# Row sums on VectorE in place of TensorE matmuls for the conditioning of a two-block transformer

## Chip, cores and metric

One NeuronCore of a Trainium2 chip runs the whole program in one launch. The metric is the device time of one execution, in microseconds; the number shown for a kernel is the median of its runs.

## The reference, cut to what matters

A first block of two layers (feed-forward, a mixer, feed-forward) works on 256 tokens of 1024 features. A second block of two layers works on the same tokens and on 256 context tokens. Its norms and gates are modulated by a conditioning vector, one for the tokens (`c`) and one for the context (`c_ctx`):

```python
def adaln(cond, w, b, n_chunks):
    return jnp.split(jax.nn.silu(cond) @ w + b, n_chunks, axis=-1)
...
for layer in range(DEPTH):
    sh1, sc1, g1, sh2, sc2, g2 = (m[:, None, :] for m in adaln(c, w_mod[layer], b_mod[layer], 6))
    ...
    h_ctx = rmsnorm(ctx, norm1_g[layer]) * (1 + csc1) + csh1
    ...
    x = x + g1 * mix_lat
    x = x + g2 * channel_mixer(rmsnorm(x, norm2_g[layer]) * (1 + sc2) + sh2, ...)
```

`w_mod` is [2, 1024, 6144] in fp32, 50 MB in all. Both conditioning vectors and the context are inputs, so none of the modulation and nothing of the context's first norm but its shift and scale depends on the first block. The context's vectors are not needed for the second half of layer 1 (tiles 16 to 47 of that layer).

## The kernel before

Activations lie transposed in SBUF, features on partitions: `X` and `C` are eight tiles of 128x256. Every weight is streamed in units of 128x1024 fp32 (512 KB). SP's queue loads them in the order of use into 11 slots (`raw`, `load`, L526), up to 11 units ahead. ScalarE copies a unit into its high part `whi` (6 slots, `upto`, L1383), VectorE subtracts for the low part `wlo` (`upto`, L1872), and TensorE does three products of high and low parts. So a unit passes through four engines, each in its own fixed program order, tied by semaphores. ScalarE and VectorE run five or six units ahead of TensorE at most.

A feed-forward has 22 steps. In step f TensorE does the units gate f, up f and down f-2 (`FFN`, `ffn`, L756); two more down units end it. VectorE's part is `hidden` (L960): per step it sums the halves of the gate product, splits one unit, writes the low part of the previous product (`low`), then sums the halves of the up product, multiplies, and splits two units:

```python
dve.wait_ge(weight_used, p + n)
sum_halves(gs[:, f % 2, 0:T], 2 * f % 3).then_inc(halves_taken, 1)
upto(p + n + SPLIT - 1)
if f >= 1:
    low(f - 1)
...
upto(p + n + SPLIT + 1)
```

The line numbers of `hidden` in the profile are L1960 and on, those of `low` L1969, of the sums L1965, of the product L1992. The stages follow each other as ("ffn1", 0), ("in", 0), ("out", 0), ("ffn2", 0), the same with 1, then c0 and x0 (the second block's layer 0 mixers of context and tokens), ffc and ffx (its feed-forwards), c1in, x1in and the rest of x1, and last the experts (L1213), which nothing here touches. Between two stages stands a norm (`norm`, L727 on TensorE, L1402 on ScalarE, L1890 on VectorE): ScalarE squares eight tiles, TensorE sums them over partitions, ScalarE takes the root, VectorE inverts it and scales. In ("ffn2", l) the taps of a long filter are computed besides, in 17 steps that go from engine to engine (`filter_step`, L1049, L1581, L2142); GpSimd loads its tables behind the first unit (`filter_tables`, L624).

Modulation (`modulate`, L734) is a product on TensorE with the two conditioning vectors as the stationary operand `CS` and w_mod as the moving one, in 6 groups of 16 tiles of 128x1024. SP's queue loads the tiles among the weights (`mods`, L542). Group 0 and group 2 run around the norm behind ("ffn1", l), group 1 around that in front of ("ffn1", 1), group 3 at the end of the first block, group 4 inside ffc (after up 13 and up 20), group 5 inside ffx (after up 13) and behind c1in. ScalarE copies each group's rows to `MR` (`rows_out`, L1421), TensorE turns them with four transposes (`turn_rows`, L745) and VectorE adds the bias (`take_rows`, L1914).

The first block ends with its final norm of `X`. Then `scales` computes the gains, and `mix2("c0")` begins with the norm of `C`, whose output its first unit needs tile by tile. In ffc and ffx the norm of the next input is done in passing (`side_step`, L1433, L1948): ScalarE squares in steps 1 to 8, GpSimd adds the eight tiles into one (`fold`, L637), TensorE sums that over partitions after up 9 (`side_sum`, L752).

## Time and profile before

| | |
|---|---|
| runs shown | 3026.64, 3025.33, 3030.46 us; median 3026.64 |
| profiled execution | 3028.71 us, span 3026.9 us |
| granted TensorE clock, mean | 0.989 |
| busy share: TensorE, VectorE, ScalarE, GpSimd | 97%, 73%, 57%, 2% |
| read from HBM | 684.86 MB |
| w_mod loads | 96 of 512 KB, on SP's queue |

Times are microseconds from the first instruction of the profiled execution. The difference between its span and its own time lies before the first and after the last instruction. PE is TensorE, PEld its weight load, DVE VectorE, ACT ScalarE, POOL GpSimd. A busy time of PE counts pipelined matmuls, whose ends are modelled, so it tells whether the engine had work and not how fast it worked. The first 36% of the span is the first block; the experts begin at about 2255 us.

### The profile page before, as it was taken

The numbers are of one execution on the slowest core, as the hardware profiler recorded it, in microseconds if no ns is written. First come the engines' busy times: TensorE is split into PE (matmuls) and PEld (weight loads), VectorE is DVE, ScalarE is ACT, GpSimd is POOL, SyncE is SP. The second block draws the span as 40 slices with busy tenths as digits, with TensorE's granted clock in tenths as the row PEclk, the third lists the DMA queues.
The fourth block names the chain that finished last, engine by engine and source line by source line (L and its number), as shares of the span: only waits on it lengthen the run. The fifth ranks groups of instructions, "written<-read, shape, count | busy, mean of one in ns | idle before, by whom it ended". The sixth has DMA issues, their size and how long they took to land.

```text
span 3026.9 us, 50706 instructions
## 1 busy us (share of the span) xinstructions
PE 2930.8 (97%) x18747; PEld 2566.4 (85%) x18747; DVE 2213.8 (73%) x2981; ACT 1722.7 (57%) x2379; POOL 75.4 (2%) x103
## 2 busy tenths in 40 slices
PE   8999999999999999999999999999989999999998
PEld 7989788899888888789889888997978888888887
DVE  6667666666677666566676767765678999999998
ACT  4446544444555345445544444455468788878886
POOL 2000000000000000000000000000000000000000
PEclk9999999999999999999999999999999999999999
DMA  8864465886536593565386776745559999999999
GB/s 248 276 184 140 116 194 175 260 276 184 163 117 182 159 288 92 147 178 153 93 250 183 225 237 184 224 110 149 169 196 363 366 355 363 366 362 358 364 364 336
DMA packets 664466, 692.13 MB, mean 229 GB/s; under 512 B 22830, under 2 KB 518146, under 8 KB 663009
## 3 DMA queue, kind: packets, MB, share of 16 engines
q1 hardware_dynamic: 658432, 665.06, 68.7%
q0 software_dynamic: 5712, 24.54, 2.2%
q8 instruction: 124, 2.03, 0.3%
q14 instruction: 54, 0.43, 0.1%
q10 hardware_dynamic: 144, 0.07, 0.0%
HBM read 684.86 MB, written 4.72 MB: 228 GB/s over the span
## 4 chain that ended last, share of the span: by engine, by line
PE 88%; DVE 6%; ACT 3%; issue 2%; DMA 1%; DVEq 0%; SPq 0%; ACTq 0%
PE W L693 35%; PE ACC L693 20%; PE W L786 16%; PE W L787 8%; PE W L686 4%; PE ACC L686 3%; DVE wlo L1877 2%; ACT whi L1390 1%; PE ACC L1000 1%; PE W L1210 1%; DMA scratch<-in_w_mod 1%; PE ACC L1201 0%; DVE R L1896 0%; DVE M L2030 0%; DVE gs L1965 0%
## 5 line engine op out<-in xcount | busy, mean ns | idle before, releaser
L1877 DVE TENSOR_TENSOR wlo<-raw,whi 128x1024 fp32r<-128x1024 f32 (+3 forms) x681 | 765.5, 1144 | 360.1 <-ACT whi L1390 358.1
L1390 ACT ACTIVATE whi<-raw 128x1024 fp32r<-128x1024 f32 (+3 forms) x681 | 655.5, 985 | 52.0 <-PE W L693 33.2
L2386 DVE TENSOR_TENSOR wlo<-raw,whi 128x1024 fp32r<-128x1024 f32 x528 | 617.5, 1219 | 43.5 <-ACT whi L1746 34.6
L786 PE MATMUL W<-HB,whi 128*128 128x512 f32 x1760 | 635.6, 403 | 14.0 <-DVE HB L1899 14.0
L1746 ACT ACTIVATE whi<-raw 128x1024 fp32r<-128x1024 f32 x528 | 547.4, 1060 | 94.6 <-PE W L693 52.4
L787 PE MATMUL W<-HB,wlo 128*128 128x256 f32 x1760 | 497.1, 282 | 0.0
L693 PE MATMUL W<-HB,whi 128*128 128x256 f32 x2592 | 479.4, 287 | 13.8 <-DVE HB L1899 8.0
L693 PE MATMUL W<-whi,HB 128*128 128x512 f32 (+1 forms) x1664 | 478.7, 373 | 4.9 <-issue 3.5
L693 PEld LDWEIGHTS W<-HB,whi 128*128 128x128 f32 x2592 | 407.1, 193 | 22.1 <-issue 12.7
L786 PEld LDWEIGHTS W<-HB,whi 128*128 128x128 f32 x1760 | 333.4, 189 | 103.1 <-issue 19.7
L1460 ACT ACTIVATE sg<-gs 128x256 f32<-128x256 f32 x132 | 55.1, 418 | 591.4 <-DVE gs L1965 591.4
L693 PE MATMUL W<-HB,wlo 128*128 128x256 f32 x1296 | 368.2, 284 | 0.0
L693 PEld LDWEIGHTS W<-whi,HB 128*128 128x128 f32 x1664 | 300.1, 189 | 60.3 <-DVE wlo L2386 4.4
L787 PEld LDWEIGHTS W<-HB,wlo 128*128 128x128 f32 x1760 | 336.1, 191 | 0.0
L693 PE MATMUL W<-wlo,HB 128*128 128x512 f32 (+1 forms) x832 | 307.7, 370 | 0.0
L693 PE MATMUL ACC<-hhi,whi 128*128 128x256 f32 x1056 | 303.9, 288 | 0.0
L693 PE MATMUL ACC<-hlo,whi 128*128 128x256 f32 x1056 | 298.9, 283 | 0.0
L693 PE MATMUL ACC<-hhi,wlo 128*128 128x256 f32 x1056 | 298.8, 283 | 0.0
L693 PEld LDWEIGHTS W<-HB,wlo 128*128 128x128 f32 x1296 | 250.3, 193 | 0.0
L1965 DVE TENSOR_REDUCE gs<-W 128x256 f32<-128x512 f32 x132 | 91.0, 689 | 162.2 <-PE W L787 162.1
L693 PEld LDWEIGHTS ACC<-hhi,whi 128*128 128x128 f32 x1056 | 200.6, 190 | 10.3 <-issue 4.8
L693 PEld LDWEIGHTS ACC<-hlo,whi 128*128 128x128 f32 x1056 | 200.8, 190 | 2.4 <-issue 2.4
(459 smaller groups left out, 4042.8 us busy)
## 6 DMA issues: line engine op xcount, KB each, us to landing
raw<-in_moe_w_gate SPq DMA_DIRECT2D x183, 512.0 KB, 5.3
raw<-in_moe_w_up SPq DMA_DIRECT2D x180, 512.0 KB, 5.4
raw<-in_ffn_w_in SPq DMA_DIRECT2D x176, 512.0 KB, 3.9
raw<-in_moe_w_down SPq DMA_DIRECT2D x176, 512.0 KB, 5.5
raw<-in_w_in SPq DMA_DIRECT2D x105, 512.0 KB, 4.8
raw<-in_ffn_w_out SPq DMA_DIRECT2D x88, 512.0 KB, 3.6
scratch<-in_w_mod SPq DMA_DIRECT2D x60, 512.0 KB, 7.4
raw<-in_mix_w_in SPq DMA_DIRECT2D x48, 512.0 KB, 3.7
```

The source lines that it names most:

```text
L686: return mm(o, a, b, start=start, stop=stop, skip_group_check=True)
L693: last = mm(o, a, b, start=start and i == 0, stop=stop and i == 2, skip_group_check=True)
L786: mm(o, wh[:, w], both(k), start=k == 0, stop=False, skip_group_check=True)
L787: last = mm(o[:, 0:T], wl[:, w], high[:, k, :], start=False, stop=k == KT - 1, skip_group_check=True)
L1000: last = nc.tensor.transpose(bank(4 + b % 2)[:, w], P2[:, (4 * i + b) % 3, w], ident[:, :])
L1210: last = nc.tensor.transpose(W[:, 2 * (g % 2), at], hdt[:, g % 2, at], ident[:, :])
L1390: A_(whi[:, g % SPLIT, 0:LONG[g]], raw[:, g % RAW, 0:LONG[g]], ACT.Copy).then_inc(weight_high, 1)
L1460: A_(sg[:, f % 2, 0:T], gs[:, f % 2, 0:T], ACT.Silu).then_inc(gated, 1)
L1746: A_(whi[:, g % SPLIT, :], raw[:, g % RAW, :], ACT.Copy).then_inc(weight_high, 1)
L1877: V.tensor_tensor(wlo[:, g % RAW, 0:LONG[g]], raw[:, g % RAW, 0:LONG[g]], whi[:, g % SPLIT, 0:LONG[g]].bitcast(F32), ALU.subtract).then_in ...
L1965: return V.tensor_reduce(o, W[:, b, :].rearrange("p (i t) -> p t i", i=2), AX.X, ALU.add)
L2386: V.tensor_tensor(wlo[:, g % RAW, :], raw[:, g % RAW, :], whi[:, g % SPLIT, :].bitcast(F32), ALU.subtract).then_inc(weight_split, 1)
```

## The change

w_mod comes transposed, so that a tile has 128 outputs on partitions and the 1024 inputs in the row. VectorE multiplies a tile with the conditioning vector, which stands on every partition, and sums along the row: one instruction per tile and vector. There are 96 tiles; the first 64 need both vectors, the other 32 only the tokens'. `MOD_STEPS` gives each tile a step of a feed-forward; the first half of a tile's work comes at the end of step f, the second after the gate sum of step f+1. GpSimd's queue loads the tiles into three slots, or one in ("ffn2", l), and loads the two conditioning vectors four times, since their place is used otherwise in between. ScalarE applies the Silu to them. All modulation matmuls, their row copies and transposes go.

The context's first norm moves into ("ffn2", 1): squares in steps 13 and 14, the fold on GpSimd behind the eighth tile's load, the sum after up 18, the root in step 19, the scaling in steps 20 and 21, high and low parts behind the last up unit. TensorE goes from the last down unit into c0in. The final norm of `X` moves into c0in: the squares in front, the fold on GpSimd, the sum ahead of the third unit, the scaling in units 3 to 6. The bias of layer 0 is added in step 1 of ("ffn2", 1), that of layer 1 in front of ffx and in x1in. The copy of the filter to HBM moves behind the tile loads of its stage.

```diff
+        COND = M[:, 2048:4096].rearrange("p (i k) -> p i k", i=2)
+        def mod_slot(name, i):
+            s = 0 if name in FILTERS else i % 3
+            if s == 0:
+                return s, M[:, 4096:5120]
+            return s, (G if name[0] == "ffn1" else S)[:, s * 1024:(s + 1) * 1024]
...
+        MOD_STEPS = {("ffn1", 0): range(5, 22), ("ffn2", 0): range(2, 19, 2), ("ffn1", 1): range(0, 22),
+                     ("ffn2", 1): range(2, 19, 2), "ffc": range(2, 22), "ffx": range(2, 21)}
+        COND_AT = {("ffn1", 0): 3, ("ffn2", 0): 2, ("ffn2", 1): 2, "ffc": 1}
...
@@ sync: every stream() loses its mods
-                       {RAW - 1: [(1, MODS, 16)], 24: [(2, 0, MODS)]} if l else {30: [(0, 0, MODS)]})
+                stream(("ffn1", l), ffn_units(w1, w1, FF, w2))
...
@@ gpsimd
+            def condition():
+                for i, v in enumerate((A["c_2"][0], A["c_ctx_2"])):
+                    pool.dma_start(COND[:, i, :], v.partition_broadcast(128)).then_inc(cond_in, 16)
+            def mod_tiles(name, first, last):
+                for i in range(first, last):
+                    s, dst = mod_slot(name, i)
+                    u = MOD_FIRST[name] + i
+                    if i >= (1 if name in FILTERS else 3):
+                        pool.wait_ge(mod_used, u if name in FILTERS else u - 2)
+                    elif i == 0 and u:
+                        pool.wait_ge(mod_used, u)
+                    if name == ("ffn1", 1) and i == 1:
+                        pool.wait_ge(weight_used, start[name] + 1)
+                    pool.dma_start(dst, A["w_mod_laid"][u // 48, u % 48 * 128:u % 48 * 128 + 128, :]).then_inc(mod_landed[s], 16)
...
             for l in range(2):
+                if l == 0:
+                    condition()
+                mod_tiles(("ffn1", l), 0, len(MOD_STEPS["ffn1", l]))
                 filter_tables(("ffn2", l), l)
+                condition()
+                mod_tiles(("ffn2", l), 0, 8)
+                if l == 1:
+                    fold(flat, side_squares, KT, side_folded)
+                mod_tiles(("ffn2", l), 8, 9)
+                keep_filter(l)
+            fold(flat, last_squared, KT, last_folded)
             for inst, l, full in MIXES:
                 if inst == "c1":
-                    for e in (1, 2):
-                        fold(e, TT[:, :, :].rearrange("p k t -> p (k t)"))
+                    pool.wait_ge(weight_used, start["ffc"] + 1)
+                    condition()
+                    for name in SIDE_INPUT:
+                        mod_tiles(name, 0, 10)
+                        fold(flat, side_squares, KT * SIDE[name] + KT, side_folded)
+                        mod_tiles(name, 10, len(MOD_STEPS[name]))
...
@@ tensor: ffn, mix2 and the order of the stages
                         if f == 13:
                             pe.wait_ge(side_root, e + 1)
-                            modulate(e + 3, 0, 4, W[:, 3, :])
-                        if f == 20 and name == "ffc":
-                            modulate(4, 4, KT, W[:, 3, :])
+                    if name == ("ffn2", 1) and kind == "up" and f == 18:
+                        pe.wait_ge(freq_taken, 10)
+                        side_sum(SIDE[name], W[:, 3, 0:T])
...
+                    if inst == "c0" and n == 2:
+                        pe.wait_ge(last_folded, 1)
+                        f32(ACC[:, 6, :], ones[:, :], TT[:, 0, :]).then_inc(pe_to_act, 1)
...
-                modulate(2 * l, 0, 2, W[:, 3, :])
                 norm()
-                modulate(2 * l, 2, KT, W[:, 3, :])
                 mix1(l)
                 norm(o=ACC[:, 0, :])
                 ffn(("ffn2", l))
-            modulate(3, 0, 2, W[:, 3, :])
-            norm()
-            modulate(3, 2, KT, W[:, 3, :])
+            pe.wait_ge(side_root, 1)
             mix2("c0")
...
@@ scalar: ffn and mix2
+                    if COND_AT.get(name) == f:
+                        act.wait_ge(cond_in, 32 * list(COND_AT).index(name) + 32)
+                        A_(COND[:, :, :], COND[:, :, :], ACT.Silu).then_inc(cond_ready, 1)
...
                 high(NF - 1)
+                if name == ("ffn2", 1):
+                    act.wait_ge(weight_used, p + at[("up", NF - 1)] + 1)
+                    for k in range(KT):
+                        side_high_part(SIDE[name], k)
...
                 if inst == "c0":
-                    rows_out(3, W[:, 3, :])
+                    for k in range(KT):
+                        act.wait_ge(dve_to_act, heard.next("dve_to_act"))
+                        A_(TT[:, k, :], X[:, k, :], ACT.Square).then_inc(last_squared, 1)
...
@@ vector
+            def mod_part(name, f, i):
+                if f not in MOD_STEPS[name]:
+                    return
+                j = MOD_STEPS[name].index(f)
+                u = MOD_FIRST[name] + j
+                both = u < 64
+                if i == 1 and not both:
+                    return
+                s, w = mod_slot(name, j)
+                if i == 0:
+                    dve.wait_ge(mod_landed[s], 16 * mod_load(name, j))
+                    if u:
+                        dve.wait_ge(mod_used, u)
+                    if j == 0 and name in COND_AT:
+                        dve.wait_ge(cond_ready, list(COND_AT).index(name) + 1)
+                ins = V.scalar_tensor_tensor(w if i or not both else JUNK, w, 1.0, COND[:, i, :], ALU.mult, ALU.mult,
+                                             accum_out=MOD[:, u // 48, u % 48, i:i + 1])
+                if i == 1 or not both:
+                    ins.then_inc(mod_used, 1)
...
+            def early_step(f):
+                if f == 1:
+                    add_bias(0, 0, 48, True)
+                    for w in range(2):
+                        scales(0, w)
+                if f == 20:
+                    dve.wait_ge(side_root, 1)
+                    link(V.reciprocal(R[:, :], R[:, :]))
+                if f in (20, 21):
+                    for k in range(4 * (f - 20), 4 * (f - 19)):
+                        side_scale(0, k)
...
                     sum_halves(gs[:, f % 2, 0:T], 2 * f % 3).then_inc(halves_taken, 1)
+                    mod_part(name, f - 1, 1)
                     upto(p + n + SPLIT - 1)
...
                     upto(p + n + SPLIT + 1)
+                    mod_part(name, f, 0)
                 low(NF - 1)
+                mod_part(name, NF - 1, 1)
+                if name == ("ffn2", 1):
+                    for k in range(KT):
+                        side_low(SIDE[name], k)
                 upto(p + N + AHEAD - 1)
...
+                    if n == 3 and inst == "c0":
+                        dve.wait_ge(act_to_dve, heard.next("act_to_dve"))
+                        link(V.reciprocal(R[:, :], R[:, :]))
+                    if 3 <= n < 7 and inst == "c0":
+                        for k in (2 * n - 6, 2 * n - 5):
+                            done_x = V.scalar_tensor_tensor(X[:, k, :], X[:, k, :], PV[:, 3, 74 + k:75 + k], R[:, :],
+                                                            ALU.mult, ALU.mult)
```

## Rows read from the trace of the kernel before

**Rows 1.** The page's busy line: busy us (share of the span) xinstructions.
```profile
PE 2930.8 (97%) x18747; PEld 2566.4 (85%) x18747; DVE 2213.8 (73%) x2981; ACT 1722.7 (57%) x2379; POOL 75.4 (2%) x103
```

**Rows 2.** Busy time by stretch, most of ("ffn1", 1); columns as in the first line.
```profile
core 0: us, PE busy (x) PEld busy (x) DVE busy (x) ACT busy (x) POOL busy (x), PEclk, DMA share, GB/s
586.00:772.00 186.00, 186.00 (x1227) 169.85 (x1225) 122.96 (x160) 79.98 (x113) 0.00 (x0) 1.00 0.72 220
```

**Rows 3.** Chain of waits in order of time: start, us, what.
```profile
205.65 8.63 PE ACC L693 x72
...
561.97 8.64 PE ACC L693 x72
...
763.64 8.64 PE ACC L693 x72
...
1126.37 5.52 PE W L686 x32
...
1146.69 8.81 PE W L693 x48
1155.50 0.44 PE ACC L749 x4
...
1691.88 3.57 PE W L686 x32
```

**Rows 4.** Timeline of VectorE, one step of ("ffn1", 1): start, us, what [idle before <-releaser].
```profile
675.59 0.69 DVE L1965 TENSOR_REDUCE gs<-W 128x256 f32<-128x512 f32 x1 [1.52 <-PE W L787]
677.72 1.23 DVE L1877 TENSOR_TENSOR wlo<-raw,whi 128x1024 fp32r<-128x1024 f32 x1 [1.44 <-ACT whi L1390]
...
680.26 2.35 DVE L1877 TENSOR_TENSOR wlo<-raw,whi 128x1024 fp32r<-128x1024 f32 x2
684.11 0.69 DVE L1965 TENSOR_REDUCE gs<-W 128x256 f32<-128x512 f32 x1 [1.50 <-PE W L787]
```

**Rows 5.** Timeline of TensorE, the norm in front of ("ffn2", 0), without modulation.
```profile
353.59 3.62 PE L686 MATMUL ACC<-TT,ones 128*128 128x256 f32 x16
361.17 0.77 PE L786 MATMUL W<-HB,whi 128*128 128x512 f32 x1 [3.97 <-DVE HB L1899]
...
366.79 0.40 PE L786 MATMUL W<-HB,whi 128*128 128x512 f32 x1
```

**Rows 6.** Busy time behind that norm, columns as in rows 2.
```profile
361.00:370.00 9.00, 8.83 (x35) 6.95 (x36) 6.89 (x17) 6.82 (x11) 2.75 (x6) 0.69 0.20 58
```

**Rows 7.** Timeline of TensorE behind the three norms with modulation.
```profile
226.99 0.38 PE L693 MATMUL W<-HB,whi 128*128 128x256 f32 x1
...
586.90 0.40 PE L786 MATMUL W<-HB,whi 128*128 128x512 f32 x1
...
783.74 0.39 PE L693 MATMUL W<-HB,whi 128*128 128x256 f32 x1
```

**Rows 8.** Groups by line: count, busy us, mean ns, idle before.
```profile
L1896 DVE RECIPROCAL R<-R 128x256 f32<-128x256 f32 x9 | 15.8, 1752 | 21.2 <-ACT R L1414 21.2
L2367 DVE SCALAR_TENSOR_TENSOR TT<-ACC,now,scratch 128x1024 f32<-128x1024 f32 x8 | 10.3, 1284 | 10.6 <-PE ACC L693 10.6
L1571 ACT ACTIVATION_READ_ACCUMULATOR M<-W,small 128x1 f32 x48 | 9.7, 202 | 0.0
```

**Rows 9.** Timeline of VectorE, the scaling by the final norm.
```profile
1134.21 3.25 DVE L1903 SCALAR_TENSOR_TENSOR X<-X,PV,R 128x256 f32<-128x256 f32 x8
```

**Rows 10.** Timeline: the sum after up 9 of ffc, and the fold in ffx.
```profile
1657.19 0.59 PE L686 MATMUL W<-TT,ones 128*128 128x256 f32 x2
...
1844.82 5.15 POOL L641 TENSOR_TENSOR TT<-TT 128x1024 f32<-128x1024 f32 x3 [190.76 <-ACT TT L1438]
```

**Rows 11.** Timeline of ("ffn2", 0): the table's load, the sine, a 1024-column pass.
```profile
371.99 0.59 POOL L633 DMA_DIRECT2D scratch<-in_k_dft  x1
...
383.17 0.42 ACT L1585 ACTIVATE scratch<-gscratch 64x256 f32<-64x256 f32 x1 [2.80 <-DVE gscratch L2140]
...
389.74 1.04 ACT L1588 ACTIVATE gscratch<-gscratch 128x1024 f32<-128x1024 f32 x1
```

**Rows 12.** DMA issues from 365 to 390: count, KB each, us to landing.
```profile
scratch<-in_k_dft POOLq DMA_DIRECT2D x1, 1408.0 KB, 10.6
```

More of the change, by code:

```diff
@@ L694, in mm3, with linear @@
                 return last
-            def linear(p, units, x, to, by_tile=None, group=None, off=0, free=None, ahead=None, drain=True):
+            def linear(p, units, x, to, by_tile=None, off=0, free=None, ahead=None, drain=True):
                 N = len(units)
                 for n, (kt, nn) in enumerate(units):
-                    if group is not None and n == 2:
-                        turn_rows(group, ACC4[:, 0, :])
                     if ahead is not None:
@@ L1299, in _ @@
             ffn("ffc")
-            ffn("ffx", 4)
+            ffn("ffx")
             ctx_keys_values()
@@ L1793, in _ @@
                 ffn(("ffn2", l))
-            norm(X, after="tiles", ahead=start["c0in"] + AHEAD)
             mix2("c0", 0)
@@ L2002, in summed, with ffn @@
                     dve.wait_ge(weight_used, start[name] + sizes[name])
-            def ffn(name, gate, res, group=None, tiles=True):
-                hidden(name, group)
+            def ffn(name, gate, res, tiles=True):
+                hidden(name)
                 for n in range(KT):
@@ L2328, in mix2 @@
                 if inst == "x0":
[L2329 removed]
+                    side_low(SIDE["x0"], KT - 1)
             def ctx_keys_values():
```

243 lines of the change are left out of this document (103 added, 140 removed).

## The prediction, made before the changed kernel ran

> **What bounds the kernel now.** I read the page's busy line first: TensorE is busy for 97% of the span [rows 1]. The split by stage says the same of the feed-forwards of the first block and leaves VectorE at two thirds there [rows 2]. So a microsecond taken out of TensorE's order counts where its neighbours run back to back, and VectorE has room for work, but not much more than a third of a step. Next, the chain of waits in order of time shows where modulation stands on the path: 5.52 us right at the end of the first block, and 3.57 us three times inside the second block's feed-forwards, between matmuls that wait for nothing [rows 3]. Last, the timeline of one steady step of a feed-forward gives VectorE's own schedule [rows 4]: a step is 8.52 us (675.59 to 684.11), of which VectorE waits 1.44 us for ScalarE's high part and 1.50 us for the next gate unit. That leaves 5.58 us of work. A down unit is 8.64/3 = 2.88 us [rows 3], so gate and up take 2.82 us each.
>
> **Removed: modulation between the stages.** A norm without it has a row: from 353.59 (end of the unit before) to 366.79 (end of the first unit behind it) is 13.20 us; TensorE idles 3.97 us, and the first unit behind the wait lasts 5.62 us (361.17 to 366.79), 2.8 more than the 2.82 of a steady one [rows 5]. The granted clock is 0.69 on average from 361 to 370 [rows 6]: for that unit it is at the lower of its two levels, 1.2 in place of 2.4 GHz. With modulation the same stretch runs from 214.28 to 226.99 + 2.88 = 229.87 (15.6 us), from 570.61 to 586.90 (16.3 us) and from 772.28 to 783.74 + 2.88 = 786.62 (14.3 us) [rows 3, 7]. So 2.4, 3.1 and 1.1 us come off, not the 5.5 us that TensorE spends, because most of it filled a wait of the norm, and the low clock after an idle wait is already in the 13.20. Two of the three follow a stage whose last tile has two VectorE instructions behind the last up unit; they make the residual later by about a microsecond, of which I let 0.5 us through in each. Gain 5.6 us.
>
> **Removed: modulation inside ffc and ffx.** Three pieces of 3.57 us [rows 3] with nothing idle beside them: 10.7 us. The fourth, ahead of x1in, fills a wait for the norm: nothing. The six sets of four transposes take 0.44 us on the chain [rows 3], in ffn nearer 0.36: 2.3 us. A sum added to ("ffn2", 1) costs an eighth of the norm's 3.62 us [rows 5]: -0.5 us.
>
> **The boundary to c0.** Now 1126.37 to 1155.50 holds two units (5.76 us) and 23.4 us of two norms, modulation and low clock [rows 3]. After the change the context's tiles are scaled in steps 20 and 21 of ("ffn2", 1), so c0in can follow the last down unit. Three things remain. (a) Steps 20 and 21 load VectorE with a reciprocal (1.75 us [rows 8]) and twice four scalings of 3.25/8 = 0.41 us [rows 9], ahead of the last product: step 20 has 5.58 + 1.44 + 3.4 = 10.4 us against 8.52, step 21 starts 1.9 us late and adds 1.6 us. The low part for the last down unit is ready 7.9 us behind the last up unit, and TensorE wants it at 2 x 2.88 = 5.76: 2.1 us idle. (b) The residual update of X stands on VectorE behind eight low parts, so it ends about 4.5 us after the last down unit; ScalarE squares, GpSimd folds in 5.15 us [rows 10], and TensorE waits for the fold ahead of the third unit, 5.76 us in: 10.1 - 5.8 = 4.3 us idle. (c) An idle stretch of that length cost 2.8 us of low clock behind it [rows 5], and the sum itself is 0.5. Together 9.7 us; gain 23.4 - 9.7 = 13.7 us. Scaling X afterwards lies in VectorE's gaps of c0in.
>
> **Added: 160 multiply-and-sum instructions on VectorE**, 128x1024, two per tile for 64 tiles and one for 32. No row shows one with a sum output. The nearest without is 1.28 us on 128x1024, and ScalarE's read of an accumulator is 0.20 us [rows 8], so 1.28 to 1.48 us; I take 1.3, as two subtractions of the size follow each other at 2.35/2 [rows 4]. In ("ffn1", l) the second one of a tile lands in the 1.44 us gap and the first in the 1.50 us gap [rows 4]: free up to 1.44 us, and 5.58 + 2 x 1.3 = 8.2 us of 8.52 are then filled. In ffn2 a tile comes every second step. What hides them is thus VectorE's gap alone; each 0.1 us beyond 1.5 costs 0.2 us per step in 39 steps. By the Trainium skill (Vector Engine (DVE) Microarchitecture Reference, "Points that are easy to get wrong") a scalar_tensor_tensor with two SBUF sources that aren't bf16 runs at half throughput. By that the sum would end slower; it is the last rival.
>
> **Moved: the loads, from SP's queue to GpSimd's.** 96 transfers of 512 KB as before, at about 0.6 us of issue each [rows 11]. SP's queue loses its waits, which held up no weights. On GpSimd they stand ahead of the folds, and a load waits for VectorE to free its slot. That matters once in ffc: its tenth load waits for tile 7 (step 8), whose second instruction runs in step 9, 0.7 + 1.3 us behind the end of gate 9. With the issue the fold starts 2.7 us behind that point and ends 5.15 us later, at 7.9; TensorE wants the sum right behind up 9, at 2.8. Before, the sum ran at 1657.19 without a wait [rows 10]. So 5.1 us idle and 2.8 us of low clock: -7.9 us. In ffx tiles have one instruction and the slot comes free 2.8 us earlier: -2.1 us, and no low clock. In ("ffn2", 1) the sum is asked for three steps later: 0.
>
> **Added: two broadcast loads of the conditioning vectors and a Silu of them**, four times. In ffn2 they stand behind the filter's tables on GpSimd's queue. The table issued at 371.99 takes 10.6 us to land [rows 11, 12], to 382.6, so 1 MB behind it lands near 390 at the same rate (1408 KB in 10.6 us) and near 387 if half of that time was not its own, and ScalarE, which asks for it in step 2, just behind the sine at 383.17 [rows 11], stands 4 to 6 us and then computes 2 us on 2048 columns (twice the 1.04 us for 1024 at 389.74 [rows 11]). Weight high parts queue behind it. They are five units ahead, which covers most; I take 2.5 us of TensorE idle in each of the two, from bounds of 0 (the depth covers all) and 8 (nothing). -5 us. In ("ffn1", 0) and ffc the loads have time or the delay is under the depth: 0, at most 2.
>
> **Sum.** 5.6 + 10.7 + 2.3 - 0.5 + 13.7 - 7.9 - 2.1 - 5.0 = 16.8 us. The profiled execution took 3028.71 us, span 3026.9; it would take 3011.9. The median of the runs shown is 2.07 us lower: **3010 us**.
>
> **Rivals.**
> *The waits aren't paid.* The vectors land in time, and the depth of weights takes the folds' delay at c0. Back come 5 us and some 3 of c0: 3002 us. For it: a step is 8.5 us and five units are 14. Against: GpSimd works in order.
> *VectorE a little over its step.* At 1.6 us per instruction both gaps overflow, 0.27 us per step; over 22 and 17 steps, less 0.8 us of margin at each end (the last low part is ready at 5.0 us of 5.76), 9 us: 3019 us.
> *VectorE is the bound, slower than before.* The place is ("ffn1", l) from step 5 and step 0 on. Between 256 and 1024 columns the rows give (1.28 - 0.41)/768 = 1.13 ns per column; at twice that an instruction takes 2.45 us, a step 5.58 + 4.9 = 10.5 us, 2.0 us over, 39 times 77 us, and 7 steps of ffc some 9 more: about 3096 us. It decides from 39 x (5.58 + 2c - 8.52) = 18.3 (the gain and the two margins), c = 1.70 us. Against: the scalings have two fp32 SBUF sources and take 0.41 us on 256 columns, where half rate would need 0.67.
> *It doesn't take the work away.* Nothing in the diff leaves a modulation matmul on TensorE; no chance given.
>
> **Numbers.** My forecast 0.55, waits not paid 0.17, a little over 0.17, VectorE the bound 0.08; the rest is a stall that I don't see, on either side of no change (0.03). Range 2999 to 3026: down to the unpaid waits with step 20 of ("ffn2", 1) unpaid besides, up to 1.6 us per instruction with 5 us more in ffn2 and 2 in the other stages. A measurement here can tell 0.2%, 6 us, from no change. Below 3020.6: 0.82; within: 0.08; above: 0.10.
>
> **What the profile would show.** No matmul with the conditioning operand; TensorE busy about 40 us less. The new instruction at 1.2 to 1.44 us, and gate sums of ("ffn1", 1) every 8.5 us; if they come every 9 us or more, the third rival. From the last down unit of ("ffn2", 1) to the third unit of c0in about 15 us with one idle stretch ended by ScalarE or GpSimd. An idle stretch of about 5 us ended by the fold behind up 9 of ffc, 2 us in ffx. ScalarE idle in step 2 of ffn2 until the vectors land. Wrong would be: the same distances between boundaries, or idle TensorE in steady steps.

## The result, and the profile after

The kernel after the change takes 3038.78 us (median of seven runs, 3034.53 to 3045.65), the kernel before 3026.95 us on the same chip: measured ratio 1.0043, 95% interval 1.0033 to 1.0053 (the two medians alone give 1.0039). It is 0.4% slower where I forecast 0.55% faster, and outside my range. The profiled execution is the slowest of the seven, 3045.65 us with a span of 3043.8; its span is 16.9 us longer than before's, the median 11.8, so some 5 us of what the comparison of traces shows are this execution's own.

The page's busy line after, which answers to [rows 1], and the row of its queues that grew (packets, MB, share of the DMA engines' time; 5712 packets and 24.54 MB before):

```profile
PE 2908.9 (96%) x18311; PEld 2574.4 (85%) x18311; DVE 2399.6 (79%) x3294; ACT 1727.4 (57%) x2377; POOL 143.8 (5%) x213
q0 software_dynamic: 20688, 79.07, 7.4%
```

TensorE has 436 instructions less, yet its busy time fell by 21.9 us only, where I had expected about 40, and the mean granted clock of the core went from 0.989 to 0.977. To see what that means I added up half-microsecond windows from the first weight matmul (20.5 us) to the start of the second block's expert part (2226.98 us before, 2241.24 after). Idle is the window less the busy time; "lost to the clock" is busy time times one minus the granted clock; the remainder is TensorE's work at full clock. A matmul that waits a little for its operand inside a unit counts as busy, so the lost time is an upper bound of what the clock cost; e4_clock_fill below shows a place where it cost nothing.

| us of TensorE | before | after | difference |
|---|---|---|---|
| work at full clock | 2116.4 | 2062.4 | -54.0 |
| idle | 67.9 | 106.8 | +38.9 |
| lost to the low clock | 22.2 | 51.5 | +29.3 |
| length | 2206.5 | 2220.7 | +14.3 |

So the change does what it says: 54.0 us of work are gone. 38.9 come back as waits and up to 29.3 as low clock behind them. By stretch, against my terms (plus is a gain; the lengths run from first matmul to last):

| stretch | before | after | gain | forecast |
|---|---|---|---|---|
| ("ffn1", 0) | 193.8 | 197.4 | -3.6 | 0 |
| three boundaries, last down unit to end of the next unit | 47.3 | 40.8 | +6.5 | +5.6 |
| mixing of the first block, both | 260.4 | 258.8 | +1.6 | +0.8 |
| ("ffn2", 0) | 209.4 | 215.5 | -6.1 | -2.5 |
| ("ffn1", 1) | 185.2 | 184.8 | +0.4 | +0.4 |
| ("ffn2", 1) | 209.8 | 220.8 | -11.1 | -5.1 |
| last down unit to the norm of x0 | 223.8 | 208.3 | +15.5 | +16.2 |
| x0, to ffc | 226.7 | 226.8 | 0 | 0 |
| ffc and ffx | 391.6 | 407.2 | -15.6 | +1.1 |
| the rest | | | -4.5 | +0.4 |

The waits that are new, from TensorE's timeline after: start, us, what [idle before <- releaser].

```profile
51.60 0.63 PE L826 MATMUL W<-ident,scratch 128*128 128x128 f32 x4 [2.08 <-ACT C L1490]
...
423.92 1.29 PE L711 MATMUL W<-gscratch,scratch 64*128 64x512 f32 x2 [2.98 <-DVE gscratch L2205]
...
1135.75 0.36 PE L718 MATMUL ACC<-hhi,whi 128*128 128x256 f32 x1 [2.15 <-DVE hlo L2017]
1149.45 1.22 PE L711 MATMUL ACC<-TT,ones 128*128 128x256 f32 x2 [4.84 <-POOL TT L651]
...
1661.04 0.80 PE L711 MATMUL W<-TT,ones 128*128 128x256 f32 x1 [6.96 <-POOL TT L651]
...
1771.81 0.36 PE L718 MATMUL ACC<-hhi,whi 128*128 128x256 f32 x1 [2.26 <-DVE hlo L2017]
...
1862.95 0.80 PE L711 MATMUL W<-TT,ones 128*128 128x256 f32 x1 [6.58 <-POOL TT L651]
```

There are two more like them, 4.24 us at 981.50 (the filter in the second ffn2) and 2.26 us at 1973.49 (the last down units of ffx). And the low clock behind the fold of ffc, in the busy time by stretch (us, PE, PEld, DVE, ACT, POOL, PEclk, DMA share, GB/s):

```profile
1661.00:1667.00 6.00, 5.96 (x26) 5.78 (x27) 2.21 (x3) 0.00 (x0) 0.56 (x1) 0.50 0.27 87
```

TensorE is busy for 5.96 of 6 us at the lower of its two levels, so this one wait cost 6.96 us and then about 3 more.

The new instruction in its place in ("ffn1", 1), VectorE's timeline, against [rows 4]:

```profile
686.14 0.69 DVE L2013 TENSOR_REDUCE gs<-W 128x256 f32<-128x512 f32 x1 [0.35 <-PE W L790]
686.75 1.21 DVE L1939 SCALAR_TENSOR_TENSOR gscratch<-gscratch,M 128x1024 f32<-128x1024 f32 x1
687.89 0.08 DVE L1939 DVE_READ_ACCUMULATOR gscratch<-gscratch,M 128x1 f32 x1
688.27 1.22 DVE L1886 TENSOR_TENSOR wlo<-raw,whi 128x1024 fp32r<-128x1024 f32 x1 [0.30 <-ACT whi L1389]
689.41 0.42 DVE L2017 TENSOR_TENSOR hlo<-hd,hhi 128x256 fp32r<-128x256 f32 x1
689.74 0.68 DVE L2013 TENSOR_REDUCE us<-W 128x256 f32<-128x512 f32 x1
690.46 0.43 DVE L2041 TENSOR_TENSOR hd<-sg,us 128x256 f32<-128x256 f32 x1
690.80 2.35 DVE L1886 TENSOR_TENSOR wlo<-raw,whi 128x1024 fp32r<-128x1024 f32 x2
693.08 1.22 DVE L1939 SCALAR_TENSOR_TENSOR M<-M 128x1024 f32<-128x1024 f32 x1
694.22 0.08 DVE L1939 DVE_READ_ACCUMULATOR M<-M 128x1 f32 x1
694.68 0.69 DVE L2013 TENSOR_REDUCE gs<-W 128x256 f32<-128x512 f32 x1 [0.38 <-PE W L790]
```

It takes 1.22 us and 0.08 for the read of its sum: the 1.3 us of my sum. Gate sums come every 8.54 us (686.14 to 694.68), and VectorE still waits 0.38 us for TensorE: free in a steady step of ffn1, as forecast.

### The profile page after: what moved, and what is told of

Its sections match the earlier page's. It is cut to its first block, busy times and chain, and to the rows that moved or that the text cites. A ratio compares the mean times of both kernels' runs of the same rounds, so it can differ in the third digit from the quotient of the medians.

```text
span 3043.8 us, 50209 instructions
## 1 busy us (share of the span) xinstructions
PE 2908.9 (96%) x18311; PEld 2574.4 (85%) x18311; DVE 2399.6 (79%) x3294; ACT 1727.4 (57%) x2377; POOL 143.8 (5%) x213
## 4 chain that ended last, share of the span: by engine, by line
PE 77%; DVE 12%; ACT 5%; issue 3%; DMA 1%; POOL 1%; POOLq 0%; DVEq 0%; ACTq 0%; SPq 0%
PE W L718 35%; PE ACC L718 16%; PE W L789 11%; PE W L790 6%; DVE wlo L1886 5%; PE ACC L711 3%; PE W L711 3%; ACT whi L1389 2%; DVE gs L2013 1%; DMA M<-in_c_ctx 1%; PE ACC L1001 1%; DVE M L1939 1%; PE W L1214 1%; DVE us L2013 1%; DVE hlo L2017 0%
## 5 line engine op out<-in xcount | busy, mean ns | idle before, releaser
L789 PE MATMUL W<-HB,whi 128*128 128x512 f32 x1760 | 642.7, 407 | 18.1 <-DVE HB L1908 18.0
L718 PE MATMUL W<-HB,whi 128*128 128x256 f32 x2592 | 486.3, 290 | 21.6 <-DVE HB L1908 13.4
L718 PEld LDWEIGHTS W<-HB,whi 128*128 128x128 f32 x2592 | 413.2, 196 | 28.4 <-issue 19.1
L789 PEld LDWEIGHTS W<-HB,whi 128*128 128x128 f32 x1760 | 337.1, 192 | 109.8 <-issue 24.2
L790 PEld LDWEIGHTS W<-HB,wlo 128*128 128x128 f32 x1760 | 340.5, 193 | 0.0
L718 PEld LDWEIGHTS W<-HB,wlo 128*128 128x128 f32 x1296 | 254.1, 196 | 0.0
L718 PEld LDWEIGHTS ACC<-hhi,wlo 128*128 128x128 f32 x1056 | 205.6, 195 | 0.0
```

What stands on the lines that cost most here:

```text
L718: last = mm(o, a, b, start=start and i == 0, stop=stop and i == 2, skip_group_check=True)
L789: mm(o, wh[:, w], both(k), start=k == 0, stop=False, skip_group_check=True)
L790: last = mm(o[:, 0:T], wl[:, w], high[:, k, :], start=False, stop=k == KT - 1, skip_group_check=True)
```

## The experiments

Lengths and stalls are from each kernel's trace, times are medians; 3038.78 is what they are held against, with the kernel before beside each. The single kernels scatter by about 5 us to either side from run to run, so a gain of 4 us is told from nothing only just.

**The fold in ffc and ffx.**

```diff
-                        mod_tiles(name, 0, 10)
+                        mod_tiles(name, 0, 9)
                         fold(flat, side_squares, KT * SIDE[name] + KT, side_folded)
-                        mod_tiles(name, 10, len(MOD_STEPS[name]))
+                        mod_tiles(name, 9, len(MOD_STEPS[name]))
```

> One number changes: in ffc and ffx GpSimd issues nine tile loads ahead of its fold, not ten, so the fold no longer waits for VectorE to free the slot in step 9. My theory: the two stalls ended by the fold (6.96 us at 1661.04 and 6.57 us at 1862.95) and the low clock behind them (about 3 us of TensorE's time each) are the price of that wait, so both vanish and the time falls from 3038.8 to about 3019 us (3015 to 3023). The fold starts right behind ScalarE's last square, near 1645.5, and is over before up 9 ends. Rival: the sum of VectorE's work in ffc and ffx, stretched by the folds, is what the two stages pay for; then TensorE's idle time moves to the last down units (2.26 us each now, 5 or more then) and the gain is under 8 us, 3031 us or more.

Measured: 3025.48 us, ratio 0.9999 [0.9989, 1.0009], so 13.3 us better than after: outside the theory's range, between it and the rival. Both waits for the fold are gone; GpSimd starts it at 1642.49 and ends at 1649.48. But TensorE's timeline at the end of ffc has

```profile
1760.96 0.55 PE L718 MATMUL ACC<-hhi,whi 128*128 128x256 f32 x1 [4.05 <-DVE hlo L2017]
```

where it was 2.26 us, and again in ffx. VectorE's own timeline in that kernel says why:

```profile
1659.69 0.69 DVE L2013 TENSOR_REDUCE gs<-W 128x256 f32<-128x512 f32 x1
1661.82 1.23 DVE L1886 TENSOR_TENSOR wlo<-raw,whi 128x1024 fp32r<-128x1024 f32 x1 [1.44 <-ACT whi L1389]
1662.96 0.42 DVE L2017 TENSOR_TENSOR hlo<-hd,hhi 128x256 fp32r<-128x256 f32 x1
1663.30 0.68 DVE L2013 TENSOR_REDUCE us<-W 128x256 f32<-128x512 f32 x1
1664.01 0.42 DVE L2041 TENSOR_TENSOR hd<-sg,us 128x256 f32<-128x256 f32 x1
1664.36 2.35 DVE L1886 TENSOR_TENSOR wlo<-raw,whi 128x1024 fp32r<-128x1024 f32 x2
1666.63 1.22 DVE L1939 SCALAR_TENSOR_TENSOR scratch<-scratch,M 128x1024 f32<-128x1024 f32 x1
...
1667.77 0.69 DVE L2013 TENSOR_REDUCE gs<-W 128x256 f32<-128x512 f32 x1
```

No wait for TensorE is left in this step: only the one of 1.44 us for ScalarE, which itself waits for the gate sum. The cycle is 8.08 us and doesn't get shorter, TensorE's is 8.52. What VectorE has lost it makes up at 0.44 us a step.

**The conditioning vectors.**

```diff
-("ffn2", 0): range(2, 19, 2), ... ("ffn2", 1): range(2, 19, 2)
+("ffn2", 0): range(4, 21, 2), ... ("ffn2", 1): (5, 7, 9, 11, 13, 15, 17, 18, 19)
-COND_AT = {("ffn1", 0): 3, ("ffn2", 0): 2, ("ffn2", 1): 2, "ffc": 1}
+COND_AT = {("ffn1", 0): 5, ("ffn2", 0): 4, ("ffn2", 1): 5, "ffc": 1}
```

(and GpSimd issues six tiles ahead of the fold of the second ffn2, not eight)

> The Silu of the conditioning vectors stands in step 5 of ffn1 (was 3), step 4 of the first ffn2 (was 2) and step 5 of the second (was 2); the tiles of ffn2 begin in those steps, two apart as before and one apart at the end of the second. The number of instructions is the same. My theory: ScalarE's wait for the vectors and the 1.9 us Silu in the filter's steps make VectorE late for the filter's first taps, and cost TensorE 2.07, 2.98 and 4.24 us idle (51.60, 423.92, 981.50) and some 1.7 us of low clock behind each: all three vanish, the time falls by 14 us to about 3024 us (3020 to 3028). Rival: it is VectorE's multiply-and-sum instructions in the filter's steps that make it late; they are still there, so the stalls of the two ffn2 move but stay, only the 3.8 us of ffn1 go, and the time is about 3035 us.

Measured: 3030.99 us, ratio 1.0011 [1.0001, 1.0020]; 7.8 us better, where I expected 14 and a time of 3028 at most. The filter's wait falls to 0.87 us and, in the second ffn2, from 4.24 to nothing (another, for the tap sums, grows from 0.88 to 2.04). The theory holds for both ffn2, as far as this run can tell: the edit moves the first tiles together with the Silu, so it doesn't separate the two. It was wrong for ("ffn1", 0), where 2.32 us stay at 50.68 with the Silu two steps later. In the kernel after the change ScalarE's timeline shows both causes:

```profile
38.80 1.06 ACT L1389 ACTIVATE whi<-raw 128x1024 fp32r<-128x1024 f32 x1 [2.46 <-DMA raw<-in_ffn_w_in]
...
385.30 1.91 ACT L1473 ACTIVATE M<-M 128x2048 f32<-128x2048 f32 x1 [1.48 <-DMA M<-in_c_ctx]
```

At 385.30 it stands 1.48 us for the vectors and computes 1.91: VectorE, which waits for ScalarE's next high part, is 3.4 us late and reaches the filter's taps late. The two traces separate what the run doesn't: the gate sum of the next step comes 30.3 us behind the stage's first matmul (391.62) where it came at 26.3 before (387.44), and of these 4.1 us 3.4 are ScalarE's; of the multiply-and-sum instructions only one had run by then. At 38.80 ScalarE stands for a weight.

**The start.**

```diff
                 if l == 0:
+                    pool.wait_ge(weight_used, 9)
                     condition()
```

> One wait is added to the kernel after the change: GpSimd issues the first load of the conditioning vectors and the first tiles only when TensorE has used nine weights (about 46 us in). My theory: in the first 40 us these 2.5 MB share the DMA engines with the first weights of the feed-forward, one of which ScalarE waits for (2.46 us at 38.80), and that is the stall of 2.07 us at 51.60 with 1.7 us of low clock behind it. Both go: 3038.8 less 4 us, 3035 us (3032 to 3037). The vectors land near 52 us; ScalarE asks for them in step 3, at 51.4, so up to 2 us of its time may come back. Rival: the stall is ScalarE's table or VectorE's copy and not the loads: no change, or ScalarE now waits for the vectors and the stall stays: 3037 to 3042 us.

Measured: 3044.63 us, ratio 1.0055 [1.0038, 1.0072]: 6 us worse, a miss. The first half was right: with the loads held back no weight is late, and the wait at 51.60 is gone. But now the vectors are late, issued at 48.94, and TensorE stands 7.23 us at 65.28. ScalarE's timeline:

```profile
57.10 1.91 ACT L1474 ACTIVATE M<-M 128x2048 f32<-128x2048 f32 x1 [8.35 <-DMA M<-in_c_ctx]
```

It is 8.2 us from the first issue to the last landing for 1 MB among 1.5 MB of tiles and the weights. Of ScalarE's wait of 8.35 us I had allowed 2. The start needs both, later loads and a later Silu (it has them in e8_all below). In kernels that leave the start as it is, TensorE's wait there (2.08 us at 51.60 above) is 1.1 to 3.6 us long from one execution to the next: part of the scatter of this change's times.

**Order inside VectorE's step.** In every feed-forward, on both engines:

```diff
-                    upto(p + n + SPLIT - 1)
                     if f >= 1:
                         high(f - 1)
+                    upto(p + n + SPLIT - 1)
```

(on VectorE `low(f - 1)`; its second multiply-and-sum also behind `low`, and `low(f)` of the last step ahead of its last `upto`)

> In each step of every feed-forward the split of the previous hidden tile (high part on ScalarE, low part on VectorE) comes ahead of the next weights' split, and in the last step ahead of the next stage's weights. The instructions are the same. My theory: VectorE runs one wait late at the end of ffc and ffx and of the second ffn2, which costs 2.26, 2.26 and 2.15 us of idle TensorE (1771.81, 1973.49, 1135.75) and about 2 us of low clock behind each of the first two. With the low part earlier by about 1.5 us (in the wait for ScalarE) in steps and by 2.4 us at the end these go: 3028 us (3024 to 3032). The low part fills part of the 1.43 us gap, so a step of VectorE doesn't grow. Rival: the weights' low parts, now 0.4 us later, are what TensorE waits for next, idle of 0.3 us or more appears in steady steps, and the time stays or rises (3038 to 3050 us).

Measured: 3049.5 us, ratio 1.0078 [1.0061, 1.0095]: 10.7 us worse. The aimed-at waits shrank (2.26 to 0.62, 2.15 to 0.55 us), and yet. VectorE's timeline at the end of ("ffn1", 1):

```profile
769.41 0.68 DVE L2013 TENSOR_REDUCE gs<-W 128x256 f32<-128x512 f32 x1
770.88 0.42 DVE L2017 TENSOR_TENSOR hlo<-hd,hhi 128x256 fp32r<-128x256 f32 x1 [0.79 <-ACT hhi L1457]
771.23 1.22 DVE L1939 SCALAR_TENSOR_TENSOR gscratch<-gscratch,M 128x1024 f32<-128x1024 f32 x1
```

and TensorE's behind it:

```profile
782.09 0.70 PE L711 MATMUL W<-TT,ones 128*128 128x256 f32 x2 [3.28 <-ACT TT L1409]
```

The low part now stands first in the wait for ScalarE, of which 0.79 us is idle again, and the modulation instruction that had filled it comes after: gate sums now come every 8.57 us, 760.84 to 769.41, without a wait for TensorE, where they came every 8.53 with a wait of 0.37. VectorE has become the bound, arrives late at the residual, and the next norm's squares with it. Two waits for GpSimd's fold grew as well, at c0 from 4.84 to 7.09 us and in ffc from 6.96 to 9.30; how much of the 10.7 us each accounts for isn't separated. Not the weights, as my rival had it, but VectorE's cycle: in ffn1 it has 0.37 us a step to spare and no more.

**The slot of the single instruction.** On top of e1_fold_first:

```diff
-                if i == 1 and not both:
+                if i == 0 and not both:
                     return
...
-                if i == 0:
+                if i == 0 or not both:
```

> On top of e1_fold_first: where a tile has one multiply-and-sum instruction (the later tiles of ffc, all of ffx) it stands in VectorE's wait for ScalarE's high part (1.43 us, empty there) at the start of the next step, not in the slot behind the step's last low part. My theory: with the instruction in the other slot VectorE's own cycle is 8.07 us (gate sum to gate sum back to back, 1659.69 to 1667.77 in e1_fold_first) against TensorE's 8.52, so it makes up only 0.45 us per step of what the fold and the side norm cost it, and is still 4 us late at the last down units. In the wait its cycle is 6.8 us and the two stalls of 4.05 us and the low clock behind them (2 us each) go: 3025.5 less 12 us, 3013.5 us (3010 to 3018). Rival: what makes VectorE late at the end is work near the end, not the slack of a step, or the tile isn't there in time in the earlier slot: gain under 4 us, 3021 us or more.

Measured: 3016.4 us, ratio 0.9956 [0.9939, 0.9974]: 9.1 us better than e1_fold_first, as the theory had it. VectorE's step in ffc, with side work in it:

```profile
1711.85 0.68 DVE L2014 TENSOR_REDUCE gs<-W 128x256 f32<-128x512 f32 x1
1712.45 1.22 DVE L1940 SCALAR_TENSOR_TENSOR scratch<-scratch,M 128x1024 f32<-128x1024 f32 x1
...
1713.97 1.23 DVE L1886 TENSOR_TENSOR wlo<-raw,whi 128x1024 fp32r<-128x1024 f32 x1 [0.29 <-ACT whi L1389]
...
1720.21 0.69 DVE L2014 TENSOR_REDUCE gs<-W 128x256 f32<-128x512 f32 x1 [0.55 <-PE W L790]
```

The instruction costs nothing there, and soon behind the side norm VectorE waits for TensorE again. From the second unit of ffc to x1in it is 419.8 us after the change (21.1 idle, 11.5 lost to the clock), 406.2 in e1_fold_first (10.8 and 7.6) and 392.8 here (2.7 and 3.0). With these two edits the kernel beats the one before.

**The last sum at c0.**

```diff
-                        pe.wait_ge(last_folded, 1)
-                        f32(ACC[:, 6, :], ones[:, :], TT[:, 0, :]).then_inc(pe_to_act, 1)
+                        pe.wait_ge(kept_out, 32)
+                        pe.wait_ge(last_squared, KT)
+                        for k in range(KT):
+                            last = f32(ACC[:, 6, :], ones[:, :], TT[:, k, :], k == 0, k == KT - 1)
+                        last.then_inc(pe_to_act, 1)
```

(and GpSimd's fold for it goes)

> The last sum of X's squares at the boundary to c0in is made by TensorE itself from ScalarE's eight squares (eight matmuls, 3.6 us), not from GpSimd's fold (one matmul). My theory: at 1149.45 TensorE stands 4.83 us for the fold and loses 2.8 us to the low clock; the squares are there at 1142.9, before it reaches the sum, so nothing is waited for and it pays 3.1 us more of work: 3038.8 less 4.5 us, 3034 us (3031 to 3037), and the granted clock from 1149 to 1155 is 1.0. Rival: c0in waits next for the weights' low parts, which VectorE could not split while GpSimd folded (6.50 us for three at 1143.99), or for X's scaling: no gain.

Measured: 3034.75 us, ratio 1.0025 [1.0016, 1.0035]: 4.0 us better, as expected. The eight matmuls wait for nothing, and the clock behind them stays up:

```profile
1140.00:1146.00 6.00, 6.00 (x48) 5.87 (x47) 0.34 (x1) 1.89 (x3) 0.00 (x0) 1.00 0.28 68
```

**Half of VectorE's new work in ffn1.** `mod_part` returns for the second instruction in ("ffn1", l); the context's sums aren't computed there.

> The kernel after the change with the second multiply-and-sum instruction of each tile left out in the two ffn1 (39 of 160 instructions, 1.22 us each with 0.08 us for reading the sum): the context's part of the first block's modulation and a part of the second's aren't computed. Theory (that of the prediction): in ffn1 the instruction stands in VectorE's wait for ScalarE's high part and costs TensorE nothing; only the one ahead of the residual at the end of each ffn1 is felt, by under 1 us. 3037 us (3034 to 3040), and the stage from 584 to 783 keeps its 198.7 us to within 1.5 us. Rival: VectorE is the bound in ffn1 too; the 39 instructions are 48 us of its work, and at least 10 us come off: 3029 us or less.

Measured: 3034.68 us, ratio 1.0028 [1.0018, 1.0039]: 4.1 us for 48 us of VectorE's work, and ("ffn1", 1) to the next first matmul is 197.9 us against 198.7. What is gained stands behind the last step, where the norm's wait is 3.97 us (776.75) in place of 4.73. The rival, VectorE as the bound in ffn1, falls.

**The clock.** Behind the eight matmuls of `norm`:

```diff
+                for i in range(14):
+                    f32(W[:, 3, 0:128], ones[:, :], ones[:, :])
```

> Behind the eight matmuls of each norm on the main path TensorE issues 14 matmuls 128x128 of ones on ones, into a bank that nobody reads, about 3 us of work in the 4 to 4.7 us in which it waits for the normalized tiles. Nothing of the computation changes. My theory: what modulation between the stages gave, beside its result, was a TensorE that stayed at 2.4 GHz; with the filler the low clock behind the norms of the first block and of x0 goes (1.6 us of TensorE's time near 226, 1 to 2.5 us at each of the seven places): 3038.8 less about 12 us, 3027 us (3022 to 3032), and the mean granted clock rises from 0.977 to about 0.984. Rival: the clock falls for another reason than the idle wait (the stalls inside the stages), or the filler delays the first matmul behind the norm: no gain, 3036 to 3042 us.

Measured: 3036.5 us, ratio 1.0036 [1.0021, 1.0050]: 2.3 us, less than its scatter; a miss. The clock did rise, to 0.983, and 11.0 us less count as lost to it; each of the six waits filled is 3.1 us shorter. But nothing behind them comes earlier. The first unit behind the norm ahead of ("ffn1", 1), in the kernel after the change and in this one (columns as above):

```profile
584.22:589.80 5.58, 5.48 (x17) 3.44 (x18) 4.82 (x14) 4.17 (x8) 0.00 (x0) 0.69 0.00 0
```

```profile
589.25:594.82 5.57, 4.90 (x17) 2.62 (x18) 4.81 (x14) 4.16 (x8) 0.00 (x0) 1.00 0.01 3
```

The unit takes 5.58 us at a mean granted clock of 0.69 and 5.57 at 1.00 (at all six places 5.6 to 6.0 in both kernels; ahead of the second ffn2 5.66 at 0.54 and 5.57 at 1.00). VectorE hands it its eight tiles one by one, each 0.73 us behind the last (`HB<-TT,HB` starts at 589.41, 590.14, 590.87 and so on in this kernel), and TensorE follows at that pace. So neither the wait ahead of this unit nor the low clock in it had anything to give back, and the filter's wait at 427 us grew to 4.35. Filling a wait raises the clock; that pays only where the work behind it is ready and no other engine sets its pace.

**All of it.** e1, e2, e5, e6, e7 and, in the last step of the second ffn2 alone, `low(f)` ahead of `upto`:

> All of it together: e1_fold_first, e2_cond_later, e5_gap_slot, e6_start_later, e7_c0_sum, and in the last step of the second ffn2 the low part of the hidden tile ahead of the next stage's weights (2.14 us of idle TensorE at 1133.76). Theory: the stalls are separate, so the gains add up: 13.3 + 7.8 (measured) + 12 + 4 + 4.5 + 2 = 43.6 us, 2995 us (2989 to 3003), 1.0% below the kernel before. Rival: they hide one another, VectorE being near its bound in the first block too; then under two thirds of the sum arrives, 3010 us or more.

Measured: 2997.93 us, ratio 0.9896 [0.9879, 0.9912]: 40.9 us below the kernel after the change, of 43.6 summed. The 43.6 were in part expectations: what e1, e2, e5 and e7 measured adds up to 34.2, and the rest is the start, which needed both edits, and `low(f)`, which no run tried alone. No sign that the stalls hide one another. The same accounting gives 2066.0 us of work, 76.1 idle and 35.9 at most lost to the clock.

Two additions to it: twelve fillers behind each norm, and the last tile's second instruction of each ffn1 behind the residual.

> e8_all with twelve filler matmuls (ones on ones, 128x128, into a bank that nobody reads) behind each norm on the main path. Theory: in e4_clock_fill the filler brought back 13 us of low clock, but half of it ran into the stalls behind (the filter's taps, 4.35 us there in place of 2.98), and two of the fourteen came too late. In e8_all those stalls are gone and twelve fit: 2997.9 less 7 us, 2991 us (2987 to 2995). Rival: the filler costs at its end what it gives back by the clock: 2996 to 3002 us.

> e8_all with the second instruction of the last tile of each ffn1 behind the residual's update of X, not ahead of it. Theory: it stands 1.22 us ahead of the residual (771.31, residual at 773.59) and the last down unit ends at 774.5, so X could be done about 1 us earlier at each of the two boundaries, and with it ScalarE's squares and TensorE's norm: 2997.9 less 2 us, 2996 us (2993 to 2999). Rival: the instruction is waited for by the next stage's weights instead: no change or 1 us more.

> e8_all, e10_all_fill and e11_all_residual in one kernel. Theory: the filler (3.9 us against e8_all) and the later instruction (2.7 us) act at the same boundaries but on different waits, the one on the clock and the other on the residual, so most of both stays: 2992 us (2989 to 2994). Rival: with X ready earlier the twelve fillers no longer fit into the wait behind the norm, and TensorE's first unit is late by what the residual won: 2994 to 2996 us, no better than either alone.

Measured: 2993.98 us (0.9888 [0.9873, 0.9903]) with the fillers, 2995.28 us (0.9892 [0.9877, 0.9907]) with the later instruction, and 2993.98 us (0.9888 [0.9872, 0.9905]) with both, as e12_best's rival had it: together they are no better than the fillers alone. All three are within 2 us of each other and 2.7 to 4.0 below e8_all, and the intervals of all four overlap, so none of these additions is told from nothing. The clock of the last is 0.991, above the 0.989 of the kernel before.

## Why the prediction was wrong

*Removed work, boundaries.* Right. The three norms cost 13.90, 13.01 and 13.89 us where I had 13.20 with half a microsecond on two; gain 6.5 for 5.6. The difference lies in my reading of before: I added a steady 2.88 us for the unit behind the norm, or took the start of the next unit for its end, and got 46.2 us, where the ends of the units give 47.3. The reason that I gave for the 13.20 was wrong, though: I put the 5.62 us of its first unit down to the low clock, and it is VectorE's pace, as e4_clock_fill shows.

*VectorE's instruction.* Its length (1.30 us) and its being free in ffn1's steady steps were right; e9_half confirms it. The half rate that the Trainium skill states for two SBUF sources that aren't bf16 (Vector Engine (DVE) Microarchitecture Reference, "Points that are easy to get wrong") isn't seen here: 1024 columns in 1.22 us, against the 2.45 that my third rival built on it. That rival failed for the reason that I gave, with a slip in it: at half rate the scaling would need 0.70 us by my own slope, not 0.67.

*The boundary to c0.* Right: 15.5 us less 2.15 idle ahead of the last down unit are 13.4, forecast 13.7. Of its terms (a) was 2.1 and is 2.15; (b) was 4.3 and is 4.84 here, 3.4 in five of the other kernels that leave this place alone. (c) was 2.8 and 2.8 are lost there, but by luck: the row that I took it from shows VectorE's pace. e7_c0_sum took (b) and (c) away for 4.0 us.

*The fold in ffc and ffx: the step that failed first.* "In ffx tiles have one instruction and the slot comes free 2.8 us earlier: -2.1 us, and no low clock." In ffc the start was right to 0.2 us, and in ffx the slot does come free 2.2 us earlier (2.84 us ahead of TensorE's stop at 1856.37, 0.66 in ffc). What I had wrong is the length: the fold takes 7.0 us in ffc and 8.8 in ffx, not the 5.15 of [rows 10], which I had taken as fixed. GpSimd's and VectorE's timelines in ffc after the change:

```profile
1653.42 0.53 POOL L645 DMA_DIRECT2D M<-in_w_mod_laid  x1 [7.99 <-DVE M L1939]
1653.96 2.89 POOL L651 TENSOR_TENSOR TT<-TT 128x1024 f32<-128x1024 f32 x1
1658.07 2.92 POOL L651 TENSOR_TENSOR TT<-TT 128x512 f32<-128x512 f32 x2 [1.22 <-issue]
```

```profile
1654.56 2.57 DVE L2017 TENSOR_TENSOR hlo<-hd,hhi 128x256 fp32r<-128x256 f32 x1
1657.05 0.68 DVE L2013 TENSOR_REDUCE us<-W 128x256 f32<-128x512 f32 x1
1657.76 0.42 DVE L2041 TENSOR_TENSOR hd<-sg,us 128x256 f32<-128x256 f32 x1
1658.10 3.96 DVE L1886 TENSOR_TENSOR wlo<-raw,whi 128x1024 fp32r<-128x1024 f32 x2
```

and GpSimd's in ffx:

```profile
1854.08 2.42 POOL L651 TENSOR_TENSOR TT<-TT 128x1024 f32<-128x1024 f32 x1
1859.44 3.46 POOL L651 TENSOR_TENSOR TT<-TT 128x512 f32<-128x512 f32 x2 [2.94 <-issue]
```

A low part of 0.42 us takes 2.57 and ends 0.28 us behind GpSimd's first addition; two subtractions take 3.96 us for 2.35 beside the others. The Trainium skill says so (SBUF — State Buffer, "SBUF: two separate sides": a VectorE instruction with two SBUF inputs and a GpSimd one exclude each other for their whole length), and these rows agree. But that is not new. VectorE's timeline beside the fold of [rows 10], before:

```profile
1845.30 2.62 DVE L1969 TENSOR_TENSOR hlo<-hd,hhi 128x256 fp32r<-128x256 f32 x1
```

VectorE was busy there for 5.12 of the 5.15 us, such stretched times counted, and the fold had 0.15 us between its additions. After the change the last two additions are 0.7 to 1.3 us longer together, and the larger part is the idle time ahead of the second: 1.22 us in ffc, 2.94 in ffx. `fold` has a `pool.drain()` there, as before; what is new is a tile load issued right ahead of the fold. In all seven kernels that issue ten loads ahead of the fold, the second addition in ffx starts 0.96 us behind the landing of that load, which took 4.95 to 5.55 us. With a load of 3.5 to 3.9 us, in ffc, it starts 1.1 to 1.2 us behind the first addition, and at c0, with the last load 32 us or more back, 0.3 to 0.5. So the load ahead, more than VectorE's work, is what the lengths go with. It stays an inference: no run folds in ffc or ffx without one, and the 10.3 us between the additions in ("ffn2", 1), where the load lands in 3.5, isn't explained by it. Idle was 13.5 us for my 7.2, and e1_fold_first removed both waits with one number.

*The second failure: "What hides them is thus VectorE's gap alone", said of ffn1 and carried over to ffc.* I counted VectorE's work per step (8.2 of 8.52 us) as if any gap would do. In ffc and ffx a tile's only instruction stands in the slot of 1.50 us behind the step, while the 1.43 us in front of ScalarE's high part stays empty. As that wait begins at the gate sum, wherever it comes, it is part of VectorE's cycle and can't be caught up: 8.08 us. With the folds' delay and the side norm's seventeen instructions, VectorE was late for the down units: 2.26 us idle in each stage, unforecast. e5_gap_slot shows it.

*The conditioning vectors.* The step that failed is "Weight high parts queue behind it. They are five units ahead, which covers most". ScalarE's wait was shorter than I had it (1.48 us and a Silu of 1.91, for 4 to 6 and 2), but VectorE, not the depth of weights, carried the delay: it came to the filter's taps late, at 2.98 and 4.24 us idle. With them came more low clock, so the two ffn2 lost 6.1 and 11.1 us. e2_cond_later gave 7.8 back. In ("ffn1", 0) I had "0, at most 2"; it was 3.6, the loads having delayed a weight.

*The low clock.* The length of the row that I priced it from [rows 5] held for the norm, but not its cause: that unit is as long at full clock. I charged 2.8 us once for a fold and once for c0: 5.6 us in all. After the change the count of the loss grew by 29.3, of which 5.1 stand behind the three norms, where a unit is paced by VectorE. All but one of the new idle stretches have their piece behind them: 1.7 us lost behind 51.60 and 423.92, 3.2 behind 981.50, 2.8 behind 1149.45, 3.0 and 2.8 behind the folds, 1.6 and 1.7 behind the last down units, 3.4 behind x1's norm, none behind 1135.75. I had charged none where I took a stall to be small. Together: of 33.7 us between forecast and measured span, ffc and ffx are 16.7, the two ffn2 9.6, ("ffn1", 0) 3.6 and the last stages 4.9, less 1.0 by which the others came out better. In the last stages the fourth piece of modulation had kept TensorE busy ahead of x1in; 2.73 us idle and 3.4 lost to the clock took its place, where I had written "nothing". Behind 2199.50 and 2241.24 4.8 us are lost for 1.6 before, with waits as long as before (1.64 and 3.08 us); why stays open.

*The rivals.* None of mine named what happened. The one on the slow side put VectorE's load in ffn1 and at 1.7 us per instruction; it was at its bound at 1.30, but in ffc and in the filter's steps, by position. The 0.10 for slower was too low for a change with some ten new waits, most of them costed without its clock or not at all.

What wasn't tried: a fold in ffc with no tile load right ahead of it, the boundary to c0 alone in the kernel before, and the change without the early norm; its 15.5 us are read from the two traces.

## What to carry to other kernels

When work leaves the bounding engine, list every place in which that work had covered a wait, and price each new wait twice: its length, and half the time for which the engine then runs at the low clock (here 1.6 to 3.4 us for waits of 2 to 7, and nothing behind one of 2.15). Leave out the second price where another engine sets the pace of what follows, as behind a norm here. An engine's slack in a step is the bound's step less its own cycle, with the waits that move along with it counted in; side work belongs in these waits, and putting a 1.3 us instruction there, not in the other gap, was worth 9 us. In a queue that works in order, count what stands ahead of the one item that somebody waits for: one tile load ahead of the folds of two stages cost 13.3 us, where the modulation matmuls in them had cost 10.7.

## What the runs showed of the hardware

A multiply with a sum output on VectorE, 128x1024 from two fp32 SBUF sources, takes 1.22 us, no longer than a subtraction of the size, and 0.08 us for the read of the sum. GpSimd's fold of 1792 columns takes 5.15 us with no load ahead of it, 6.2 at c0, and 7.0 to 8.8 in ffc and ffx right behind a tile load. It stretches VectorE's instructions from 0.42 to 2.57 us (2.62 in the kernel before) and from 2.35 to 3.96. TensorE's first unit behind a norm takes 5.58 us at a granted clock of 0.69 and 5.57 at 1.00. The two 512 KB broadcast loads of a vector to 128 partitions took 8.2 us together at 48.94 in e6_start_later, about as long as a step of the feed-forward.
